# First four up units of the convolutional MLP computed in two passes over the row tiles, with five unread matmuls ahead of them

## The chip, the cores and the metric

The kernel runs on one core of a Trainium2 chip. The metric is the device time of one execution in microseconds (us). All engines work from their own in-order instruction streams and meet at semaphores: TensorE (PE, with its weight loads as PEld), VectorE (DVE), ScalarE (ACT), GpSimd (POOL) and SyncE (SP), which here only issues DMAs.

## What is computed

One layer (layer 0) on a sequence of 256 rows of width 2048, in float32: a mixer (mLSTM), then a gated MLP, each behind an RMS norm with a shift and a scale that come from a conditioning vector, and each added back with a gate.

```
sh1, sc1, g1, sh2, sc2, g2 = split(silu(c) @ w_mod + b_mod, 6)
x = x + g1 * mlstm_mixer(rms_norm(x) * (1 + sc1) + sh1)
hf = rms_norm(x) * (1 + sc2) + sh2
u = hf @ w_up                                   # 2048 -> 2 * 5632 columns
u = sum(pad(u)[:, j:j + 256] * conv_w[j] for j in range(3)) + conv_b
gate, val = split(u, 2)
x = x + g2 * ((silu(gate) * val) @ w_down)      # 5632 -> 2048
```

## The kernel before

**Split products.** Each float32 product is made from rounded halves. A weight tile in `raw` is rounded by ACT into `w_hi` (line 609) and DVE subtracts to make `w_lo` (line 975); the activations are split likewise into `hm_hi` and `hm_lo`, which lie side by side in `hm`. A row tile k is 128 of the 2048 rows of a weight matrix.

**Up units.** One unit is 128 output columns of `w_up`, that is 16 row tiles of 128x128, 1 MB. It has two halves of 8 row tiles. Units come in fours: gate and value columns of two pairs. Unit r of a four sums into PSUM bank 4 + r. Per row tile PE runs one matmul with 512 columns (`w_hi` against `hm_hi` and `hm_lo`, `up_hi`, line 1285) and one with 256 columns (`w_lo` against `hm_hi`, `up_lo`, line 1291). In the texts unit 0 is the first up unit, unit 4 the first of the second four, and so on.

**Buffers.** `raw` holds four units. `w_hi` and `w_lo` hold four halves each. ACT rounds a half when PE has finished the one four halves earlier (`half_done`). SP loads a unit into `raw` when DVE has finished both halves of the unit that lay there (`raw_done`).

**What ACT and DVE do for each unit.** ACT copies half of the bank to `up_sum` (line 930), DVE adds the other half (1241), ACT applies the middle tap and bias (935), DVE adds two taps (1245, 1250). After a pair ACT has applied Silu to the gate (925) and DVE multiplies (`act_hi`, 1257), POOL does the low part (589, 593). Between these steps stand the roundings and subtractions of coming weight halves, in a fixed order. Once in four units DVE also adds one row tile of the modulation matrix for g2 (`add_g2`, 1224, 128x2048), which SP loads (448) and which must be done before SP issues the next such load.

**Entry of the MLP.** PE ends the mixer's output projection, sums columns of `acc` (1395), transposes the last quarter of x (1552), and spreads the row of 1/rms over all partitions (1587). DVE then multiplies each row tile of x by it (`normalise`, 1201), ACT adds the shift and rounds (`hm_hi`, 892), DVE makes `hm_lo` (`shift_lo`, 1206). PE takes row tile k as soon as it is there: `first_up_units` runs units 0 and 1 together, k from 0 to 15, then `up_unit` runs units 2 and 3, then a loop runs fours. In the first pass of DVE's loop `add_g2` stands at r == 2, ahead of the addition for unit 2.

Of the kernel before, what the change touches and what calls it, by code (L numbers as in the profile page):

```python
# [5 lines left out]
def hybrid_mlstm_convffn_adaln_kernel(nc, x_d, c_d, w_mod, b_mod, w_in, gate_bias, h_norm, w_out,  # L6
# [5 lines left out]
    ds = bass.ds  # L12
# [44 lines left out]
    PAIR0 = F_TILE  # L57


    C_SH1, C_SC1, C_G1, C_SH2, C_SC2, C_G2 = (D * n for n in range(6))  # L60
# [31 lines left out]
    with ExitStack() as ctx:  # L92
# [242 lines left out]
        def _(sp):  # L335
# [263 lines left out]
        def _(act):  # L599
            def split_hi(v, plus=0):  # L600

                if v >= 2 * N_UNITS:
                    return
                if v < V_OUT:
                    act.wait_ge(half_in[v % 8], 16 * (v // 8 + 1))
                elif v % 2 == 0:

                    act.wait_ge(raw_in[v // 2 % 4], 16 * ((v - V_OUT) // 8 + 1) + 2 * plus)
                nc.scalar.activation(w_hi[:, v % 4, :], raw_half(v), ACT.Copy).then_inc(w_hi_made, 1)  # L609

            def slot_hi(p):
# [291 lines left out]
            def seed_y(n, q):  # L903
# [6 lines left out]
                for t in range(TB):  # L910
                    nc.scalar.activation(ps[:, 2 * (q % 2) + t, :],
                                         y_acc[:, t, q * QUARTER:(q + 1) * QUARTER], ACT.Copy)\
                             .then_inc(y_seeded, 1)

            for n, tiles in enumerate(CHUNKS):
                with act.Fori(0, tiles // 2) as i:
                    for r in range(4):
# [51 lines left out]
        def _(dve):  # L969
            def split_lo(v, plus=0):  # L970

                if v >= 2 * N_UNITS:
                    return
                dve.wait_ge(w_hi_made, v + 1 + plus)
                nc.vector.tensor_tensor(w_lo[:, v % 4, :], raw_half(v),  # L975
                                        w_hi[:, v % 4, :].bitcast(f32), ALU.subtract)\
                         .then_inc(raw_done, 1)

# [191 lines left out]
            for f in range(31):  # L1170
                split_lo(V_OUT + f + 3)
                attend(V_OUT + f - V_VO)
# [24 lines left out]
            split_lo(V_OUT + 34)  # L1197

# [13 lines left out]
            for k in range(KT + 2):  # L1212
                if k < KT:
                    normalise(k)
                if k >= 2:
                    shift_lo(k - 2)
                if k == 4:
                    split_lo(V_OUT + 35)

            def add_g2(tile, plus):  # L1220
# [5 lines left out]
                                               op0=ALU.mult, op1=ALU.add).then_inc(mod_done, 1)  # L1226

            for n, tiles in enumerate(CHUNKS):
                with dve.Fori(0, tiles // 2) as i:
                    for r in range(4):  # L1230
                        u, k = U_UP[n] + r, r // 2
                        w = 2 * F_TILE[n] + r
                        pair = F_TILE[n] + k
                        buf = (conv_val if r % 2 else conv_gate)[:, k, :]
                        col = 2 * i + (FT if r % 2 else 0) + pair
# [3 lines left out]
                        dve.wait_ge(low_taken, 4 * i + w + 1)  # L1239
                        total = up_sum[:, r % 2, :]  # L1240
                        nc.vector.tensor_tensor(total, ps[:, 4 + r, 0:SEQ], total, ALU.add)\
                                 .then_inc(up_made, 1)
                        split_lo(2 * u + 5, 8 * i)
                        dve.wait_ge(conv_base, 4 * i + w + 1)
                        nc.vector.scalar_tensor_tensor(out=buf[:, 1:SEQ], in0=total[:, 0:SEQ - 1],
                                                       scalar=cvT[:, ds(col + 2 * FT, 1)],
                                                       in1=buf[:, 1:SEQ], op0=ALU.mult, op1=ALU.add)\
                                 .then_inc(tap1_made, 1)
                        dve.wait_ge(tap1_made, 4 * i + w + 1)
                        nc.vector.scalar_tensor_tensor(out=buf[:, 2:SEQ], in0=total[:, 0:SEQ - 2],  # L1250
                                                       scalar=cvT[:, ds(col, 1)],
                                                       in1=buf[:, 2:SEQ], op0=ALU.mult, op1=ALU.add)\
                                 .then_inc(conv_done, 1)
                        if r % 2:
                            dve.wait_ge(silu_made, 2 * i + pair + 1)
                            dve.wait_ge(conv_done, 4 * i + w + 1)
                            nc.vector.tensor_tensor(act_hi[:, ds((2 * i + k) * SEQ, SEQ)],  # L1257
                                                    conv_gate[:, k, :], conv_val[:, k, :], ALU.mult)\
                                     .then_inc(act_hi_made, 1)
                groups = tiles // 4  # L1260
# [17 lines left out]
        def _(pe):  # L1278
# [312 lines left out]
            def first_up_units(u):  # L1591

                pe.wait_ge(raw_done, RAW0 + 2 * u + 3)
                for k in range(KT):
                    pe.wait_ge(hm_made, KT + k + 1)
                    if k == KT // 2:
                        pe.wait_ge(raw_done, RAW0 + 2 * u + 4)
                    for r in range(2):
                        up_hi(r, 2 * (u + r) + k // (KT // 2), k)
                    for r in range(2):  # L1600
                        last = up_lo(r, 2 * (u + r) + k // (KT // 2), k, stop=(k == KT - 1))
                        if r == 0 and k in (KT // 2 - 1, KT - 1):
                            last.then_inc(half_done, 1)
                last.then_inc(half_done, 2)
# [59 lines left out]
```

## Time and profile before

| | us |
|---|---|
| median of 3 runs | 1191.35 |
| lowest and highest | 1190.84 and 1191.42 |
| the profiled execution | 1191.6 |
| its span, first to last instruction | 1189.9 |
| mean granted clock of TensorE | 0.986 |
| TensorE busy | 1164.7 (98% of the span) |
| VectorE busy | 915.8 (77%) |
| ScalarE busy | 629.7 (53%) |
| GpSimd busy | 160.8 (14%) |

Times in the trace count from the first instruction. A busy engine isn't always one at full pace: the clock that TensorE is granted is shown beside its busy time. Idle time of an engine that nobody waits for costs nothing. Matmuls overlap, so their pace is the distance of their starts, not their duration.

### The profile page before, as it was taken

Reading aid. Unit: us, or ns where it says so; the run is one execution under the profiler, and the core shown is the slowest. Engines: PE = TensorE matmul, PEld = TensorE weight load, DVE = VectorE, ACT = ScalarE, POOL = GpSimd, SP = SyncE. Lnnn points to the kernel's source line nnn. Section 1 sums busy time; section 2 is a strip of 40 time slices with the busy share of each in tenths; the row PEclk is TensorE's granted clock in tenths of the full one; section 3 lists DMA queues with packets and bytes.
Section 4 is the critical chain, followed back from the end, with each engine's and each line's share of the span. In section 5 each row is a group of like instructions: output and inputs, shape, how many; then the busy total and the mean of one; then the engine's idle time right before and its main releaser. Section 6 shows DMA issues by size and latency. Waiting matters only on the chain.

```text
span 1189.9 us, 17137 instructions
## 1 busy us (share of the span) xinstructions
PE 1164.7 (98%) x5890; PEld 995.7 (84%) x5890; DVE 915.8 (77%) x984; ACT 629.7 (53%) x915; POOL 160.8 (14%) x167
## 2 busy tenths in 40 slices
PE   5799999999999999999999999999999999999998
PEld 5788888888888888888888888888888888888887
DVE  5799877989889988988886446888885456777654
ACT  4355565665654546555554445455454555555442
POOL 0000030111112320112211000211211000221200
PEclk9599999999999998999999999999999999999999
DMA  9999989999999993897875578789775566666552
GB/s 363 398 401 402 391 288 333 358 404 401 346 352 347 401 301 101 253 251 216 254 235 193 196 216 240 215 231 253 221 222 201 191 198 179 194 192 180 204 175 77
DMA packets 260440, 314.54 MB, mean 264 GB/s; under 512 B 6208, under 2 KB 186888, under 8 KB 251688
## 3 DMA queue, kind: packets, MB, share of 16 engines
q1 hardware_dynamic: 259360, 312.51, 78.6%
q0 software_dynamic: 592, 1.22, 0.4%
q8 instruction: 28, 0.46, 0.2%
q10 hardware_dynamic: 442, 0.21, 0.1%
q14 instruction: 18, 0.15, 0.0%
HBM read 311.80 MB, written 2.11 MB: 264 GB/s over the span
## 4 chain that ended last, share of the span: by engine, by line
PE 95%; DMA 2%; SPq 1%; DVE 1%; POOL 0%; ACT 0%; issue 0%; DVEq 0%
PE ps L1285 27%; PE ps L1291 14%; PE ps L1325 9%; PE ps L1327 9%; PE ps L1326 9%; PE ps L1372 8%; PE ps L1374 7%; PE ps L1373 7%; DMA m<-in_l_w_mod_dram 2%; PE ps L1395 1%; SPq L373 1%; DVE acc L1005 0%; POOL small L543 0%; PE ps L1501 0%; PE ps L1455 0%; PE ps L1343 0%
## 5 line engine op out<-in xcount | busy, mean ns | idle before, releaser
L975 DVE TENSOR_TENSOR w_lo<-raw,w_hi 128x1024 fp32r<-128x1024 f32 x392 | 482.2, 1232 | 179.6 <-ACT w_hi L609 177.8
L609 ACT ACTIVATE w_hi<-raw 128x1024 fp32r<-128x1024 f32 x392 | 414.4, 1057 | 359.2 <-PE ps L1327 165.4
L1285 PE MATMUL ps<-hm,w_hi 128*128 128x512 f32 x1408 | 340.8, 392 | 1.8 <-DVE hm L1206 1.8
L1285 PEld LDWEIGHTS ps<-hm,w_hi 128*128 128x128 f32 x1408 | 258.8, 189 | 50.9 <-issue 2.0
L1291 PEld LDWEIGHTS ps<-hm,w_lo 128*128 128x128 f32 x1408 | 183.7, 192 | 8.8 <-DVE w_lo L975 0.2
L1291 PE MATMUL ps<-hm,w_lo 128*128 128x256 f32 x1408 | 186.0, 283 | 0.0
L1372 PE MATMUL ps<-w_hi,hm 128*128 128x512 f32 x384 | 155.0, 404 | 3.2 <-DVE hm L1025 2.7
L1374 PE MATMUL ps<-w_hi,hm 128*128 128x512 f32 x384 | 150.5, 392 | 0.0
L1373 PE MATMUL ps<-w_lo,hm 128*128 128x512 f32 x384 | 150.3, 391 | 0.0
L1327 PE MATMUL ps<-w_hi,act_lo 128*128 128x512 f32 x344 | 133.8, 389 | 0.0
L1326 PE MATMUL ps<-w_lo,act_hi 128*128 128x512 f32 x344 | 133.8, 389 | 0.0
L1325 PE MATMUL ps<-w_hi,act_hi 128*128 128x512 f32 x344 | 133.8, 389 | 0.0
L589 POOL TENSOR_TENSOR act_full<-conv_gate,conv_val 128x256 f32<-128x256 f32 x44 | 32.6, 740 | 555.7 <-DVE conv_val L1250 555.7
L930 ACT ACTIVATE up_sum<-ps 128x256 f32<-128x256 f32 x88 | 33.5, 380 | 106.5 <-PE ps L1285 104.2
L1372 PEld LDWEIGHTS ps<-w_hi,hm 128*128 128x128 f32 x384 | 72.7, 189 | 19.4 <-DVE hm L1025 2.8
L1373 PEld LDWEIGHTS ps<-w_lo,hm 128*128 128x128 f32 x384 | 72.7, 189 | 15.4 <-issue 1.0
L1374 PEld LDWEIGHTS ps<-w_hi,hm 128*128 128x128 f32 x384 | 72.5, 189 | 15.7
L987 DVE SCALAR_TENSOR_TENSOR acc<-mod_raw,cT,acc 128x2048 f32<-128x2048 f32 x32 | 76.1, 2377 | 7.0 <-issue 4.4
L1326 PEld LDWEIGHTS ps<-w_lo,act_hi 128*128 128x128 f32 x344 | 64.6, 188 | 13.5
L1327 PEld LDWEIGHTS ps<-w_hi,act_lo 128*128 128x128 f32 x344 | 64.6, 188 | 13.4
L1325 PEld LDWEIGHTS ps<-w_hi,act_hi 128*128 128x128 f32 x344 | 64.6, 188 | 13.3
L593 POOL TENSOR_TENSOR act_lo<-act_full,act_hi 128x256 f32 x44 | 65.1, 1479 | 23.7 <-DVE act_hi L1257 23.7
(172 smaller groups left out, 1085.4 us busy)
## 6 DMA issues: line engine op xcount, KB each, us to landing
raw<-in_l_w_up_dram SPq DMA_DIRECT2D x88, 1024.0 KB, 5.8
raw<-in_l_w_in_dram SPq DMA_DIRECT2D x96, 512.0 KB, 11.9
mod_raw<-in_l_w_mod_dram SPq DMA_DIRECT2D x48, 1024.0 KB, 7.9
raw<-in_l_w_down_dram SPq DMA_DIRECT2D x44, 1024.0 KB, 5.0
m<-in_l_w_mod_dram SPq DMA_DIRECT2D x32, 640.0 KB, 13.6
raw<-in_l_w_out_dram SPq DMA_DIRECT2D x16, 1024.0 KB, 8.8
m<-in_l_w_mod_dram SPq DMA_DIRECT2D x16, 768.0 KB, 13.3
mod_third<-in_l_w_mod_dram SPq DMA_DIRECT2D x8, 1024.0 KB, 8.4
```

The lines of the kernel that those rows point to most:

```text
L593: nc.gpsimd.tensor_tensor(act_lo[:, part], act_full[:, k, :], act_hi[:, part].bitcast(f32), ALU.subtract)\
L609: nc.scalar.activation(w_hi[:, v % 4, :], raw_half(v), ACT.Copy).then_inc(w_hi_made, 1)
L975: nc.vector.tensor_tensor(w_lo[:, v % 4, :], raw_half(v), w_hi[:, v % 4, :].bitcast(f32), ALU.subtract)\
L987: nc.vector.scalar_tensor_tensor(out=part, in0=src, scalar=cT[:, ds(tile, 1)], in1=part, op0=ALU.mult, op1=ALU.add).then_inc(mod_done, 1)
L1285: return mm(ps[:, 4 + w % 4, :], w_hi[:, v % 4, j * P:(j + 1) * P], both, start=(k == 0), stop=stop, skip_group_check=True)
L1291: return mm(ps[:, 4 + w % 4, 0:SEQ], w_lo[:, v % 4, j * P:(j + 1) * P], hm_hi[:, k, :], start=False, stop=stop, skip_group_check=True)
L1325: mm(out, s_hi, hi, start=first, stop=False, skip_group_check=True)
L1326: mm(out, s_hi, lo, start=False, stop=False, skip_group_check=True)
L1327: last = mm(out, s_lo, hi, start=False, stop=final, skip_group_check=True)
L1372: mm(out, s_hi, hi, start=(k == 0), stop=False, skip_group_check=True)
L1373: mm(out, s_hi, lo, start=False, stop=False, skip_group_check=True)
L1374: last = mm(out, s_lo, hi, start=False, stop=(k == final), skip_group_check=True)
```

## The change

1. **PE, five unread matmuls** of 128x512 (`o_hi` by `o_hi`, into bank 5) stand behind the spread of the 1/rms row.
2. **PE, two passes.** Units 0 and 1 together on row tiles 0 to 7 (`two_units(0, 0)`), then unit 2 and unit 3 on row tiles 0 to 7 (`unit_half`), then the same on 8 to 15. For row tile 0 the 512 columns are two matmuls of 256, so that `hm_hi` is used before `hm_lo` is there.
3. **ACT and DVE, order of halves.** The first eight halves are split in the order 0, 2, 4, 6, 1, 3, 5, 7 (`FIRST_HALVES`, `first_hi`, `first_lo`). Eight, not five, are split before the loop of fours.
4. **ACT and DVE, first pass taken out of the loop** (`take_up`, `convolve`): the four units' sums are taken one after the other with one half to split in each, and `add_g2(0, 0)` comes behind the fourth.
5. **SP**: the loads of units 4 to 7 wait for the first four second halves; the order of loads is the same.

```
-            with sp.Fori(0, KT // 2 - 1) as i:
+            load_g2(0)
+            for r in range(4):
+                sp.wait_ge(raw_done, RAW0 + V_UP + 5 + r)
+                load(U_UP[0] + 4 + r, a_src(w_up, 2 * P + P * (r // 2) + (F if r % 2 else 0)), KT)
+            with sp.Fori(1, KT // 2 - 1) as i:
...
+            def first_hi(c):
+                act.wait_ge(half_done, V_UP + c - 3)
...
             for f in range(33):
                 if f == 31:
                     squares(3, 0)
+                if f < 29:
+                    slot_hi(V_OUT + f)
+                else:
+                    first_hi(f - 29)
                 if f == 32:
                     squares(3, 1)
                     take_z(3)
                     scale_shift(4, 12, ps[:, 1, 0:KT], shift_p[:], False)
                     act.wait_ge(sc_made, 6)
-                slot_hi(V_OUT + f)
...
+                if k in (9, 10):
+                    first_hi(k - 5)
+            first_hi(6)
+            first_hi(7)
...
-                if k == 4:
-                    split_lo(V_OUT + 35)
+                if k in (4, 10, 11):
+                    first_lo({4: 3, 10: 4, 11: 5}[k])
+            first_lo(6)
+            first_lo(7)
...
+            for r in range(4):
+                take_up(0, r, 0)
+                split_lo(V_UP + 8 + r)
+                convolve(0, r, 0)
+            add_g2(0, 0)
...
             last.then_inc(rstd_row, 1)
+            for _ in range(5):
+                mm(ps[:, 5, :], o_hi[:, 0:P], o_hi[:, 0:QUARTER], start=True, stop=True)
...
-            first_up_units(U_UP[0])
-            for r in range(2, 4):
-                up_unit(U_UP[0] + r, r)
+            two_units(0, 0)
+            unit_half(2, 2, 0)
+            unit_half(3, 3, 0)
+            two_units(4, KT // 2)
+            unit_half(6, 2, KT // 2)
+            unit_half(7, 3, KT // 2)
+            pe.wait_ge(up_made, 1)
```

**Order on PE, behind the spread row.** Before:

```order
L1587 MATMUL ps<-rstd_diag,ones 128x128 [waits o_made,diag_made]
L1587 MATMUL ps<-rstd_diag,ones 128x128
L1285 MATMUL ps<-hm,w_hi 128x512 [waits hm_made,raw_done,y_scaled]
L1285 MATMUL ps<-hm,w_hi 128x512
L1291 MATMUL ps<-hm,w_lo 128x256 x2
```

Now, at the same place:

```order
L1651 MATMUL ps<-rstd_diag,ones 128x128 [waits o_made,diag_made]
L1651 MATMUL ps<-rstd_diag,ones 128x128
L1654 MATMUL ps<-o_hi 128x512 x5
L1667 MATMUL ps<-hm,w_hi 128x256 [waits hm_hi_made,raw_done,y_scaled]
L1355 MATMUL ps<-hm,w_lo 128x256
L1667 MATMUL ps<-hm,w_hi 128x256
L1355 MATMUL ps<-hm,w_lo 128x256
L1667 MATMUL ps<-hm,w_hi 128x256 [waits hm_made]
```

The five matmuls fill the place in which PE waited, and row tile 0 starts on `hm_hi` alone.

**Order on DVE, end of the first four units.** Before (L1257 is `act_hi` of the first pair, L1224 `add_g2`, L1241 the addition for unit 2, all in the loop's body):

```order
L1257 TENSOR_TENSOR act_hi<-conv_gate,conv_val 128x256
L974 REGISTER_ALU
L975 TENSOR_TENSOR w_lo<-raw,w_hi 128x1024 [waits w_hi_made]
L1222 ISA [waits acc_ready1]
L1223 REGISTER_ALU [waits mod_in0]
L1224 REGISTER_ALU [waits mod_done]
L1224 SCALAR_TENSOR_TENSOR acc<-mod_raw,cT,acc 128x2048
L1239 REGISTER_ALU
L1241 TENSOR_TENSOR up_sum<-ps,up_sum 128x256 [waits low_taken]
```

Now (L1283 is the addition for unit 3, L1304 `act_hi` of the second pair, L1275 `add_g2`, and behind the branch stands the loop's first split, the first half of unit 6):

```order
L1283 TENSOR_TENSOR up_sum<-ps,up_sum 128x256 [waits low_taken]
L1014 TENSOR_TENSOR w_lo<-raw,w_hi 128x1024 [waits w_hi_made]
L1292 SCALAR_TENSOR_TENSOR conv_val<-up_sum,cvT,conv_val 128x255 [waits conv_base]
L1297 SCALAR_TENSOR_TENSOR conv_val<-up_sum,cvT,conv_val 128x254 [waits tap1_made]
L1304 TENSOR_TENSOR act_hi<-conv_gate,conv_val 128x256 [waits conv_done,silu_made]
L1275 SCALAR_TENSOR_TENSOR acc<-mod_raw,cT,acc 128x2048 [waits mod_done,mod_in0,acc_ready1]
L1315 UNCONDITIONAL_BRANCH
L1315 ISA
L1014 TENSOR_TENSOR w_lo<-raw,w_hi 128x1024 [waits w_hi_made]
```

`add_g2` has moved from between the two pairs to behind both, directly ahead of the split of unit 6.

**Order on SP, first loads of the MLP.** Before:

```order
L346 DMA raw<-in_l_w_up_dram 128x16x128 [waits raw_done] x4
L457 UNCONDITIONAL_BRANCH
L457 ISA
L448 ISA [waits mod_done]
L448 DMA mod_raw<-in_l_w_mod_dram 128x2048
```

Now:

```order
L349 DMA raw<-in_l_w_up_dram 128x16x128 [waits raw_done] x4
L451 DMA mod_raw<-in_l_w_mod_dram 128x2048 [waits mod_done]
L349 DMA raw<-in_l_w_up_dram 128x16x128 [waits raw_done] x4
L464 UNCONDITIONAL_BRANCH
L464 ISA
L451 ISA [waits mod_done]
L451 DMA mod_raw<-in_l_w_mod_dram 128x2048
```

The second load for g2 (the last row) waits for the first `add_g2`, and the load of unit 8 stands behind it, as before.

## Rows read from the trace of the kernel before

**Rows 1.** The page: the chain of work that ended last, shares by engine.

```profile
PE 95%; DMA 2%; SPq 1%; DVE 1%; POOL 0%; ACT 0%; issue 0%; DVEq 0%
```

**Rows 2.** Timeline, 440 to 480 us, at PE's wait: start, duration, instruction, [idle before].

```profile
449.27 1.06 ACT L609 ACTIVATE w_hi<-raw 128x1024 fp32r<-128x1024 f32 x1
449.61 1.08 DVE L1201 TENSOR_TENSOR hm_full<-hm_full,ps 128x256 f32<-128x256 f32 x3
450.24 1.88 ACT L892 ACTIVATE hm<-hm_full,shift_p 128x256 fp32r<-128x256 f32 x4
450.76 0.48 DVE L1206 SCALAR_TENSOR_TENSOR hm<-hm_full,shift_p,hm 128x256 fp32r<-128x256 f32 x1
...
451.39 1.19 PE L1285 MATMUL ps<-hm,w_hi 128*128 128x512 f32 x2 [1.82 <-DVE hm L1206]
...
456.99 0.48 DVE L1206 SCALAR_TENSOR_TENSOR hm<-hm_full,shift_p,hm 128x256 fp32r<-128x256 f32 x1
```

**Rows 3.** Windows: stretch, length, busy PE, PEld, DVE, ACT, POOL, PEclk, DMA share, GB/s.

```profile
450.50:451.00 0.50, 0.00 (x0) 0.00 (x0) 0.43 (x2) 0.50 (x2) 0.00 (x0) 0.50 0.00 0
...
457.00:457.50 0.50, 0.50 (x4) 0.40 (x3) 0.50 (x3) 0.39 (x1) 0.00 (x0) 0.99 1.14 347
```

**Rows 4.** The chain that ended last, 430 to 520 us: start, length, work.

```profile
453.01 0.85 PE ps L1285 x2
...
474.72 3.65 PE ps L1285 x16
478.37 0.95 PE ps L1291 x8
479.36 1.21 PE ps L1291 x8
```

**Rows 5.** Timeline of ACT ahead of the entry.

```profile
446.21 0.63 ACT L851 ACTIVATE sq_junk<-x 128x512 f32<-128x512 f32 x1 [1.04 <-DVE x L1188]
```

**Rows 6.** Timeline, 461 to 476 us: the steps of one pair of units.

```profile
465.28 0.38 ACT L930 ACTIVATE up_sum<-ps 128x256 f32<-128x256 f32 x1 [2.35 <-PE ps L1291]
...
465.70 0.42 DVE L1241 TENSOR_TENSOR up_sum<-ps,up_sum 128x256 f32<-128x256 f32 x1 [1.51 <-ACT up_sum L930]
...
466.65 1.23 DVE L975 TENSOR_TENSOR w_lo<-raw,w_hi 128x1024 fp32r<-128x1024 f32 x1 [0.52 <-ACT w_hi L609]
...
467.79 0.48 DVE L1245 SCALAR_TENSOR_TENSOR conv_gate<-up_sum,cvT,conv_gate 128x255 f32<-128x255 f32 x1
...
468.42 0.48 DVE L1250 SCALAR_TENSOR_TENSOR conv_gate<-up_sum,cvT,conv_gate 128x254 f32<-128x254 f32 x1
...
468.94 0.42 ACT L925 ACTIVATE conv_gate<-conv_gate 128x256 f32<-128x256 f32 x1 [0.89 <-DVE conv_gate L1250]
...
469.26 0.36 ACT L930 ACTIVATE up_sum<-ps 128x256 f32<-128x256 f32 x1
...
473.07 0.88 DVE L1257 TENSOR_TENSOR act_hi<-conv_gate,conv_val 128x256 f32 x1 [0.21 <-DVE conv_val L1250]
473.88 1.21 DVE L975 TENSOR_TENSOR w_lo<-raw,w_hi 128x1024 fp32r<-128x1024 f32 x1
```

**Rows 7.** Timeline, 468 to 500 us: PE's last piece of the four units; `add_g2`.

```profile
474.55 3.82 PE L1285 MATMUL ps<-hm,w_hi 128*128 128x512 f32 x16
475.01 2.82 DVE L1224 SCALAR_TENSOR_TENSOR acc<-mod_raw,cT,acc 128x2048 f32<-128x2048 f32 x1
477.76 0.41 DVE L1241 TENSOR_TENSOR up_sum<-ps,up_sum 128x256 f32<-128x256 f32 x1
...
478.09 1.21 DVE L975 TENSOR_TENSOR w_lo<-raw,w_hi 128x1024 fp32r<-128x1024 f32 x1
```

**Rows 8.** The page's DMA issues (KB each, median us to landing), and a window.

```profile
raw<-in_l_w_up_dram SPq DMA_DIRECT2D x88, 1024.0 KB, 5.8
raw<-in_l_w_in_dram SPq DMA_DIRECT2D x96, 512.0 KB, 11.9
...
480.00:485.00 5.00, 5.00 (x29) 4.35 (x29) 4.41 (x7) 4.39 (x7) 0.65 (x1) 1.00 0.99 324
```

More of the change, by code:

```diff
@@ L57, in hybrid_mlstm_convffn_adaln_kernel @@
     PAIR0 = F_TILE
+    V_UP = 2 * U_UP[0]
+    FIRST_HALVES = [2 * r for r in range(4)] + [2 * r + 1 for r in range(4)]
     C_SH1, C_SC1, C_G1, C_SH2, C_SC2, C_G2 = (D * n for n in range(6))
@@ L913, in seed_y @@
                              .then_inc(y_seeded, 1)
+            for r in range(4):
+                act.wait_ge(half_done, V_UP + 5 + r)
+                if r % 2:
+                    act.wait_ge(conv_done, r)
+                    nc.scalar.activation(conv_gate[:, r // 2, :], conv_gate[:, r // 2, :], ACT.Silu)\
+                             .then_inc(silu_made, 1)
+                if r >= 2:
+                    act.wait_ge(conv_done, r - 1)
+                nc.scalar.activation(up_sum[:, r % 2, :], ps[:, 4 + r, SEQ:2 * SEQ], ACT.Copy)\
+                         .then_inc(low_taken, 1)
+                split_hi(V_UP + 8 + r)
+                act.wait_ge(up_made, r + 1)
+                col = (FT if r % 2 else 0) + r // 2
+                nc.scalar.activation((conv_val if r % 2 else conv_gate)[:, r // 2, :], up_sum[:, r % 2, :],
+                                     ACT.Identity, bias=cvT[:, ds(col + 3 * 2 * FT, 1)],
+                                     scale=cvT[:, ds(col + 2 * 2 * FT, 1)]).then_inc(conv_base, 1)
             for n, tiles in enumerate(CHUNKS):
-                with act.Fori(0, tiles // 2) as i:
+                with act.Fori(int(n == 0), tiles // 2) as i:
                     for r in range(4):
@@ L1170, in _ @@
             for f in range(31):
-                split_lo(V_OUT + f + 3)
+                if f < 29:
+                    split_lo(V_OUT + f + 3)
+                else:
+                    first_lo(f - 29)
                 attend(V_OUT + f - V_VO)
@@ L1228, in _ @@
+            for r in range(4):
+                take_up(0, r, 0)
+                split_lo(V_UP + 8 + r)
+                convolve(0, r, 0)
+            add_g2(0, 0)
             for n, tiles in enumerate(CHUNKS):
-                with dve.Fori(0, tiles // 2) as i:
+                with dve.Fori(int(n == 0), tiles // 2) as i:
                     for r in range(4):
[L1231 to L1235, printed above, removed]
+                        u = U_UP[n] + r
@@ L1238, in _ @@
                             add_g2(n * KT // 2, i)
[L1239 to L1242, printed above, removed]
+                        take_up(n, r, i)
                         split_lo(2 * u + 5, 8 * i)
[L1244 to L1259, printed above, removed]
+                        convolve(n, r, i)
                 groups = tiles // 4
@@ L1588, in _, with two_units @@
             last.then_inc(rstd_row, 1)
+            for _ in range(5):
+                mm(ps[:, 5, :], o_hi[:, 0:P], o_hi[:, 0:QUARTER], start=True, stop=True)
             pe.wait_ge(y_scaled, 4 + 8)
-            def first_up_units(u):
-                pe.wait_ge(raw_done, RAW0 + 2 * u + 3)
-                for k in range(KT):
+            def two_units(c, k0):
+                pe.wait_ge(raw_done, RAW0 + V_UP + c + 2)
+                for k in range(k0, k0 + KT // 2):
+                    if k == 0:
+                        pe.wait_ge(hm_hi_made, KT + 1)
+                        for part in range(2):
+                            if part == 1:
+                                pe.wait_ge(hm_made, KT + 1)
+                            for r in range(2):
+                                mm(ps[:, 4 + r, part * SEQ:(part + 1) * SEQ], w_hi[:, r, 0:P],
+                                   hm[:, 0, part, :], start=(part == 0), stop=False,
+                                   skip_group_check=True)
+                                if part == 0:
+                                    up_lo(r, r, 0)
+                        continue
@@ L1603, in first_up_units, with unit_half @@
+                        if k == k0 + KT // 2 - 1:
                             last.then_inc(half_done, 1)
-                last.then_inc(half_done, 2)
+            def unit_half(c, r, k0):
+                pe.wait_ge(raw_done, RAW0 + V_UP + c + 1)
+                for k in range(k0, k0 + KT // 2):
+                    up_hi(r, c, k)
+                for k in range(k0, k0 + KT // 2):
+                    last = up_lo(r, c, k, stop=(k == KT - 1))
+                last.then_inc(half_done, 1)
             act_hi3 = act_hi[:].rearrange("p (k t) -> p k t", k=16)
```

43 lines of the change are left out of this document (37 added, 6 removed).

## Prediction

> **What bounds the kernel now.** First the profile page: PE is busy for 98% of the span and carries 95% of the chain that ended last [rows 1], so a microsecond won or lost on PE is one in the total, wherever it lies. Then the timeline at the MLP's entry. It shows PE's one large wait of the late kernel: the first up matmul starts at 451.39 after 1.82 us idle, so since 449.57, ended by DVE's hm_lo of row tile 0 [rows 2]. The windows show what follows: the granted clock is 0.50 (1.2 GHz) from 450.5 at the latest, with PE idle, and back at 0.99 (2.4 GHz) from 457.0 [rows 3]. The chain [rows 4] gives the pace: two 512-column matmuls take 0.85 us at 1.2 GHz, so with two of half the columns a row tile of two units takes 1.28; at full clock 16 of the 512-column ones take 3.65 (0.228 each), 8 of the 256-column ones 0.95 (0.12 each). So a half unit is 8 x 0.348 = 2.78 us, a unit 5.57.
>
> **The entry, part by part.** The profiled execution took 1191.6, with a span of 1189.9; the median of the runs is 1191.35, 0.25 less. I sum against the profile and take off 0.25.
>
> *Row tile supply.* ACT's rounding of the fourth half ran at 449.27 and held ACT until 450.24 [rows 2]. It now stands ahead of the squares, where ACT was idle for 1.04 us waiting for x [rows 5], and that cover just holds its slot of 0.97. So hm_hi of row tile 0 comes some 0.2 us earlier, and DVE's run of row tiles starts 0.15 earlier (its three normalisations, 1.08 from 449.61, become the limit). Row tile 7 ended at 456.99 + 0.48 = 457.47; now 457.32.
>
> *PE.* The five unread matmuls take 5 x 0.228 = 1.14 us, until 450.7, inside the old idle time; they cost nothing and delay nothing, since hm_hi of row tile 0 is ready only then. If the clock holds, PE waits for row tiles, since eight of them for two units are 8 x 0.70 = 5.6 us and come at 0.73 apart, with DVE's subtraction of half 3 (1.2 us) between tiles 2 and 3. It starts row tile 7 at 457.32 + 0.15 (DVE to PE: 451.24 to 451.39, rows 2) and ends at 458.15. **If the clock falls at 450.2 all the same**, for as long as PE takes to be busy again, the loss is mostly inside these waits: at half pace PE would reach row tile 2 by 454.4, when tile 3 has just come. So the unread matmuls matter less than they seem.
>
> From 458.15 everything left of the four units is 2 x 2.78 + 5.57 + 2 x 2.78 = 16.7 us: unit 4 starts at 474.86. Halves 4 to 7 are split by about 460.6, 462.5, 467.7 and 468.9; PE wants them at 463.7 (both of the pair), 469.3 and 472.1, so nothing is late. Before, unit 4 started in the middle of the x16 piece, at 474.55 + 8 x 0.228 = 476.38 [rows 7]. **Gain at the entry 1.5 us.** It isn't the 1.8 idle plus some 2.7 lost to the slow clock, as DVE's supply of row tiles is the next limit.
>
> *ACT and DVE behind it.* Here I see the price. Before, the sums of unit 0 were whole at 465.2, and DVE's addition ran at 465.70. Now unit 0 ends with the pair of second halves, at 458.15 + 5.57 + 5.57 = 469.29; the addition runs at +0.08 +0.42 = 469.8 [rows 6]. From there the same steps follow at the same distances, with fewer splits between, but each waits for ACT in turn. From rows 6: addition to w_lo 0.95, to tap one 1.14, to tap two 0.63, to Silu 0.52, to the next up_sum copy 0.32, to the addition 0.42: 3.98 for unit 0. Unit 1: 0.95 + 1.14 + 0.63 + 0.69 (0.48 of tap two and the 0.21 before act_hi) + 0.81 = 4.22. Unit 2, whose w_lo is ready at once (0.33, rows 7): 0.33 + 1.14 + 0.63 + 0.52 + 0.32 + 0.42 = 3.36. Unit 3 again 4.22. Then add_g2 holds DVE for 2.75 (475.01 to 477.76, rows 7), and only behind it stands the w_lo of unit 6's first half, 1.22, plus 0.15 to PE: 469.8 + 3.98 + 4.22 + 3.36 + 4.22 + 2.75 + 1.37 = 489.7.
>
> PE wants it earlier. The second half of unit 5 is due at 474.86 + 5.57 + 2.78 = 483.2; its w_lo is the one behind unit 3's addition (481.36 + 0.95 + 1.37 = 483.7): **stop of 0.45**. Unit 6 is due 2.78 later, 486.45: **stop of 3.25**. Before, the nearest thing was the 1.21 in place of 0.95 us at 479.36 [rows 4], 0.25, behind the old place of add_g2; that stop goes.
>
> *SP.* The next g2 load waits for add_g2, so it went out after 477.83 (475.01 + 2.82, rows 7); now it goes out at about 488.4 + 0.3, and the load of unit 8 is queued behind it, 489.1. ACT's rounding of that half, and all that ACT and DVE do behind it, wait for the landing. A lone 1 MB load lands 5.8 us after its issue [rows 8]; with the g2 load's 1.05 MB ahead of it at 324 GB/s (3.2 us) I take 498.1. Then 1.1 for w_hi, 1.13 for w_lo, 2.75 for the second add_g2, 0.33 for the addition and 1.37 for the w_lo of unit 8's second half: 504.8, due at 489.7 + 11.14 + 2.78 = 503.6. **Stop of 1.25.** Its bounds: none when the two loads don't slow each other (landing 494.9, ACT and DVE are busy with unit 5 until 497), 4.1 when unit 8's load takes the 11.9 us of the loads in the saturated part. The single-load row is the nearer. Behind that the lead comes back: DVE was busy for only 4.41 of 5.00 us there [rows 8], so it gains on PE.
>
> The Trainium skill (DMA: Bandwidth & Descriptors, Anatomy of one DMA) puts about 2.0 us of fixed cost on a DMA, mostly receipt, beside bytes over bandwidth. With this trace's 324 GB/s it gives 488.7 + 2.0 + 6.5 = 497.2 and, an estimate, a last stop of 0.35 instead of 1.25. For one load the row has 5.8 us where the rule of the Trainium skill gives 5.2, so I stay with the row.
>
> *Nil by cover:* PE's wait for the first addition (469.8 + 0.4, wanted at 474.86); loads of units 4 and 5, now issued near 461 and 463, landing near 467 and 470, wanted at 469.7 and 475.4.
>
> **Sum:** -1.5 - 0.25 + 0.45 + 3.25 + 1.25 = +3.2 us. 1191.6 + 3.2 - 0.25 = **1194.5**.
>
> **Rivals.**
> A. The sum above: 0.48 (with its bounds 1193.8 to 1195.6).
> B. The last stop doesn't come, because the two loads overlap: +1.9, 1193.3, with its bounds 1192.3 to 1193.7. For it: the old g2 load and the load of unit 8 followed each other too, and ACT shows no wait for them. 0.20.
> C. DVE isn't late, the other side. The steps of rows 6 hold waits on ACT (0.52 before w_lo, 0.89 at Silu) in loop code with register instructions; in straight code they could shrink. If unit 6's w_lo is ready for PE by 486.0 instead of 489.7, only the entry's gain is left: -1.75, **1189.6**. It must save 3.7 of the 19.9 us since 469.8, while the waits of rows 6 end with another engine's work and not with issue. 0.14.
> D. The unread matmuls don't do what they are for and the clock stays at 0.50 until 457.0, as before. Then PE leaves the first pass 1.2 us later: at 1.28 us a row tile from 451.2 it has done four and a half by 457.0, and the rest takes 3.5 x 0.70, until 459.4. All stops behind it stay, since DVE waits for the same sums: +4.4, 1195.7. Against it: the clock came back at 457.0 after PE had worked from 451.39, and here it works from 449.5 on. 0.13.
> E. Something not in the rows, either way: 0.05.
>
> The Trainium skill (TensorE: Matmul & The Clock Gate, Part 1: The HAM clock gate) says that the moment of the clock's change isn't tied to the kernel, so that one kernel shows different counts of slow matmuls from run to run. By it D's 1.2 us would come in some executions and not in others; this is why D keeps 0.13 although the rows speak against it.
>
> **How the numbers follow.** A measurement of this kernel tells about 0.2% (2.4 us) from no change, so slower begins at 1193.7 and faster ends at 1189.0. Slower: A 0.47, D 0.13, a part of B and E 0.04: 0.64. Faster: a part of C with more than its sum, 0.03, and E: 0.04. Same: the rest, 0.32. The range must leave out at most 0.2: it drops C and the far end of the last stop, and runs from B's low bound, widened by 0.4 for the chain's steps, 1191.9, to 1196.4 (D with some of the last stop's bound).
>
> **What would show it.** Right: PE without a wait over 0.6 us from 454.6 to 483; DVE's last row tile of the first eight near 457.3; unit 4 near 474.9; then PEld or PE waiting about 3 us near 486 to 490 for w_lo, with the 128x2048 step of DVE ending just before; the next g2 load near 488.5; a second wait near 504. Wrong: no wait at 486 (C); a clock of 0.50 to 457 (D); unit 4 at 476 (the entry isn't limited as I say).

## The result

| | us, median | lowest to highest | runs |
|---|---|---|---|
| kernel before | 1191.37 | 1190.84 to 1192.64 | 6 |
| changed kernel | 1195.42 | 1194.92 to 1197.61 | 6 |

The ratio is 1.0037, with a 95% interval of 1.0027 to 1.0048. The changed kernel is slower by some 4 us, against a forecast of 1194.5.

The profile of this comparison was of the changed kernel's slowest execution (1197.61, span 1195.9; the other five spans are 1193.2 to 1193.9). A second profile, taken with the experiments (e9, below: 1196.6, span 1194.9), shows the same kernel without the early fall of the clock at the entry. I read the stages in the second one and come back to the first for the clock.

In both the last stretch of PE already starts late, ahead of everything that was changed: the first column sums, which stood at 444.57 before, start at 445.31 and 445.89. So I compare distances from these sums. On that scale 1.32 us are to be taken off the second profile's times to lay them beside the rows of before.

The page of the changed kernel (first profile), chain by engine, beside [rows 1]:

```profile
PE 93%; DMA 2%; DVE 2%; SPq 1%; ACT 1%; POOL 0%; issue 0%; DVEq 0%; ACTq 0%
```

PE's share fell from 95% to 93% and DVE's rose from 1% to 2%. The end is now set for a while by VectorE. The timeline of PE in the second profile shows where (start, duration, instruction, idle before it and what ended it):

```profile
450.65 1.41 PE L1654 MATMUL ps<-o_hi 128*128 128x512 f32 x5
...
459.56 2.01 PE L1349 MATMUL ps<-hm,w_hi 128*128 128x512 f32 x8
...
476.31 2.00 PE L1349 MATMUL ps<-hm,w_hi 128*128 128x512 f32 x8
...
485.22 1.21 PE L1355 MATMUL ps<-hm,w_lo 128*128 128x256 f32 x8 [0.39 <-DVE w_lo L1014]
...
491.16 2.50 PE L1349 MATMUL ps<-hm,w_hi 128*128 128x512 f32 x8 [2.89 <-DVE w_lo L1014]
```

The row at 459.56 is unit 2's first half, so the first pass over units 0 and 1 ends there. Unit 4 starts at 476.31, 30.42 us behind the column sums; before it was 476.38 - 444.57 = 31.81 [rows 7]. That is the gain, 1.39 us. Unit 5's second half waits at 485.22 and unit 6 at 491.16, and there the gain is lost twice over. The timeline of DVE up to that second wait:

```profile
471.22 0.43 DVE L1283 TENSOR_TENSOR up_sum<-ps,up_sum 128x256 f32<-128x256 f32 x1 [0.99 <-ACT up_sum L945]
...
475.13 0.42 DVE L1283 TENSOR_TENSOR up_sum<-ps,up_sum 128x256 f32<-128x256 f32 x1 [0.82 <-ACT up_sum L945]
...
479.25 0.41 DVE L1283 TENSOR_TENSOR up_sum<-ps,up_sum 128x256 f32<-128x256 f32 x1
...
483.00 0.43 DVE L1283 TENSOR_TENSOR up_sum<-ps,up_sum 128x256 f32<-128x256 f32 x1 [0.82 <-ACT up_sum L945]
...
487.10 2.34 DVE L1275 SCALAR_TENSOR_TENSOR acc<-mod_raw,cT,acc 128x2048 f32<-128x2048 f32 x1
489.37 1.74 DVE L1014 TENSOR_TENSOR w_lo<-raw,w_hi 128x1024 fp32r<-128x1024 f32 x1
```

These are the four additions of the peeled units (3.91, 4.12 and 3.75 apart), then `add_g2`, then unit 6's split, which PE waits for. That is the chain [rows 6, 7] were read for. After the stop the clock goes down, in the windows of the same profile (columns as in [rows 3]):

```profile
491.00:492.00 1.00, 0.84 (x4) 0.71 (x5) 1.00 (x3) 0.29 (x1) 0.00 (x0) 1.00 0.42 123
492.00:493.00 1.00, 1.00 (x5) 0.81 (x4) 0.97 (x2) 1.00 (x2) 0.00 (x0) 0.84 0.99 418
493.00:494.00 1.00, 1.00 (x5) 0.87 (x4) 0.88 (x2) 0.62 (x3) 0.00 (x0) 0.50 0.98 411
```

PE stood still until 491.16, its clock fell within 492 to 493, when it was busy again, and stayed at 0.50 (1.2 GHz) to 496.

Unit 6's first half and the first eight matmuls of its second, 24 in all, take 3.86 us from start to start at full clock (488.31 to 492.17 in e10, below); here 491.16 to 496.54 is 5.38. So the fall costs 1.52 us. The prediction had no such term.

The transfers behind it, timeline of SyncE's queue and of ACT in the second profile:

```profile
489.70 0.37 SPq L451 DMA_DIRECT2D mod_raw<-in_l_w_mod_dram  x1
490.42 4.34 SPq L349 DMA_DIRECT2D raw<-in_l_w_up_dram  x2
```

```profile
499.58 1.06 ACT L616 ACTIVATE w_hi<-raw 128x1024 fp32r<-128x1024 f32 x1 [3.72 <-DMA raw<-in_l_w_up_dram]
```

The load for unit 8 goes out at 490.42 and ACT waits 3.72 us for it. Yet PE has no wait at unit 8 here, since the slow clock has put it back by more than the data are late.

**The sum by this profile**, in starts of PE against starts: -1.39 (entry), -0.28 (the old stop at 479.36, [rows 4]), +0.54 (unit 5: its eight matmuls start at 485.22 and not at 484.68), +3.07 (unit 6: 491.16 against 488.09), +1.52 (clock) = +3.5. Further on the starts of PE are 3.69 later than before (507.68 - 445.89 against 502.67 - 444.57), so some 0.2 us is in none of these terms. The medians differ by 4.05 in the first comparison and by 3.69 in the second (1195.07 against 1191.38). The terms are those of one execution, though: how often the clock falls behind the stop in the others isn't shown, so the share of the clock in the median isn't fixed by it.

The first profile differs in one thing. Its clock fell at the entry too, in the windows:

```profile
448.00:449.00 1.00, 1.00 (x10) 1.00 (x9) 0.21 (x2) 0.88 (x3) 0.72 (x1) 0.74 0.00 0
...
454.00:455.00 1.00, 1.00 (x7) 1.00 (x6) 1.00 (x4) 0.79 (x2) 0.00 (x0) 0.50 0.00 0
455.00:456.00 1.00, 1.00 (x7) 0.92 (x7) 1.00 (x2) 0.07 (x1) 0.00 (x0) 0.85 0.00 0
```

It fell during the second column sums, before the unread matmuls, which then took 2.48 us in place of 1.41 and ended as late as 454.0. Unit 4 started 31.99 us behind the first sums (477.30 - 445.31), so the entry gained nothing in that execution. It explains most of why it was 2 us above the rest.

### The profile page after: what moved, and what is told of

It is laid out like the page before. It is cut to its first block, busy times and chain, and to the rows that moved or that the text cites. A ratio compares the mean times of both kernels' runs of the same rounds, so it can differ in the third digit from the quotient of the medians.

```text
span 1195.9 us, 17083 instructions
## 1 busy us (share of the span) xinstructions
PE 1167.4 (98%) x5897; PEld 997.6 (83%) x5897; DVE 916.7 (77%) x984; ACT 629.2 (53%) x915; POOL 158.7 (13%) x167
## 3 DMA queue, kind: packets, MB, share of 16 engines
q0 software_dynamic: 592, 1.22, 0.4%
## 4 chain that ended last, share of the span: by engine, by line
PE 93%; DMA 2%; DVE 2%; SPq 1%; ACT 1%; POOL 0%; issue 0%; DVEq 0%; ACTq 0%
PE ps L1349 26%; PE ps L1355 14%; PE ps L1389 9%; PE ps L1391 9%; PE ps L1390 9%; PE ps L1436 8%; PE ps L1438 7%; PE ps L1437 7%; DMA m<-in_l_w_mod_dram 2%; PE ps L1459 1%; SPq L376 1%; DVE w_lo L1014 1%; DVE acc L1051 0%; ACT w_hi L616 0%; POOL small L550 0%
## 5 line engine op out<-in xcount | busy, mean ns | idle before, releaser
L1014 DVE TENSOR_TENSOR w_lo<-raw,w_hi 128x1024 fp32r<-128x1024 f32 x384 | 473.2, 1234 | 181.4 <-ACT w_hi L616 179.3
L616 ACT ACTIVATE w_hi<-raw 128x1024 fp32r<-128x1024 f32 x384 | 406.0, 1058 | 359.1 <-PE ps L1391 162.9
```

The costliest lines, as they stand in the source:

```text
L1014: nc.vector.tensor_tensor(w_lo[:, v % 4, :], raw_half(v), w_hi[:, v % 4, :].bitcast(f32), ALU.subtract)\
```

## The experiments

My theory after the two profiles: the interleaved first pass is a gain; what makes the kernel slower is one stop at unit 6, made by the chain of sums and by `add_g2` ahead of that unit's split, and the fall of the clock that the stop brings. The rivals: the entry itself (unread matmuls, clock); the chain of sums alone or the addition alone; the late transfer of unit 8. All comparisons are with runs of the kernel before on the same chip (medians 1191.41, 1191.22 and 1191.38, of 27, 33 and 15 runs). The experiments are told by question and not in the order of their numbers.

**e9: the changed kernel again, for a second profile.**

> The changed kernel as it is, for a second profile: the first was its slowest execution, with the clock at 0.50 from 448.48 to 455.30. Theory: in an execution in which the clock stays up through the entry, unit 4 starts 30.4 us behind the first column sums (31.8 before), the stops of 0.38 and 2.88 us at units 5 and 6 stand as they are, and the clock falls in the latter for about 3.4 us; 1195.0 to 1195.8. Rival: without the fall at the entry the second does not come either, and the stop at unit 8's second half is there instead.

Measured: 1195.07 (1194.46 to 1197.53, 5 runs), ratio 1.0036, interval 1.0022 to 1.005. The rows above are from it. Unit 4 came at 30.42, the stops were 0.39 and 2.89, the clock fell for 3.4 us behind them, and no wait at unit 8. The rival is out: here the second fall came without the first.

**e1: `add_g2` moved ahead of the sums.**

```diff
+            add_g2(0, 0)
             for r in range(4):
                 take_up(0, r, 0)
                 split_lo(V_UP + 8 + r)
                 convolve(0, r, 0)
-            add_g2(0, 0)
```

> The changed kernel with VectorE's one add_g2(0, 0) moved from behind the four peeled sums to ahead of them, behind first_lo(7), where VectorE waits 1.00 us for PE anyway. Theory (the addition that stands directly ahead of unit 6's w_lo makes the long stop, and the stop makes the clock fall again): the stop of 2.88 us at unit 6 shrinks to about 0.5, stops of 0.4 and 1.2 come at unit 5 (the sums start 1.4 later), the next row of modulation weights is asked for earlier, so unit 8 does not wait either, and the clock is not at 0.50 near 493: -2.88 +0.5 +1.2 -1.7 = about -2.9, 1192 to 1192.6 us. Rival 1 (the entry, with its five unread matmuls and the interleaved first pass, costs the time): 1195 to 1196, no change. Rival 2 (the chain of sums itself is too slow, whatever stands ahead of unit 6): the stops at units 5 and 6 sum to 3 us or more and the time stays above 1194.5.

Measured: 1191.54 (1190.94 to 1192.84, 11 runs), ratio 1.0000, interval 0.9991 to 1.0009. One instruction in another place takes back the whole loss, a little more than the 1192 to 1192.6 that I expected. Timeline of PE in e1, its wait at unit 5's second half and unit 6 behind it:

```profile
483.87 1.22 PE L1355 MATMUL ps<-hm,w_lo 128*128 128x256 f32 x8 [0.95 <-DVE w_lo L1014]
484.93 4.20 PE L1349 MATMUL ps<-hm,w_hi 128*128 128x512 f32 x16
```

The stop of 2.89 has gone. Left are 0.95 and about 0.4 inside the x16 group, which takes 4.20 where an undisturbed one takes 3.82. The clock did not fall:

```profile
486.00:487.00 1.00, 0.93 (x5) 0.43 (x3) 1.00 (x2) 0.00 (x0) 0.90 (x1) 1.00 1.05 296
488.00:489.00 1.00, 1.00 (x6) 0.79 (x6) 1.00 (x2) 1.00 (x2) 0.00 (x0) 1.00 1.08 279
```

So rivals 1 and 2 fall: neither the entry nor the sums alone keep the time up. Why e1 only equals the kernel before can be added up from starts: the entry gains 1.40 (unit 4 at 474.40 - 443.99 = 30.41) and the old stop 0.28, and against that stand 1.10 at unit 5's second half (483.87, due at 482.77), 0.10 behind it and 0.39 in the x16 group (from start to start 4.04 in place of 3.65).

**e4: PE kept busy through the stop.**

```diff
+            for r in range(4):
+                if r == 2:
+                    for _ in range(12):
+                        mm(ps[:, 0, :], hm[:, 0, 0, 0:P],
+                           hm[:, 0, :, :].rearrange("p a t -> p (a t)"), start=True, stop=True)
+                up_unit(U_UP[0] + r, r, 8)
             for n, tiles in enumerate(CHUNKS):
-                with pe.Fori(int(n == 0), tiles // 2) as i:
+                with pe.Fori(2 * int(n == 0), tiles // 2) as i:
```

> The changed kernel with twelve unread matmuls of 512 columns on PE between unit 5 and unit 6, in the stop of 2.88 us (12 x 0.228 = 2.74 us), into bank 0 that nothing reads then; the loop of the up units starts one turn later for it, and nothing else moves. Theory (the clock falls because PE stood still for 2.88 us): no 0.50 near 493, which gives back about 1.7 us, and in its place unit 8's second half waits about 1.25 us for its late transfer, as forecast: 1195.4 - 1.7 + 1.25 = about 1195.0, with the stop at unit 8 in the trace. Rival 1 (the clock falls there for another reason, at every run): it falls all the same, 1195.4. Rival 2 (unit 8's data are in time): 1193.7.

Measured: 1193.86 (1193.08 to 1196.03, 11 runs), ratio 1.0018, interval 1.0009 to 1.0027. The work that PE waits for ends as late as before: unit 6 starts 45.27 us behind the first sums (490.97 - 445.70), as in e9 (491.16 - 445.89). Timeline of PE, then a window behind it:

```profile
487.91 2.88 PE L1702 MATMUL ps<-hm 128*128 128x512 f32 x12
490.97 2.11 PE L1349 MATMUL ps<-hm,w_hi 128*128 128x512 f32 x8 [0.18 <-DVE w_lo L1014]
```

```profile
493.00:494.00 1.00, 1.00 (x11) 1.00 (x10) 1.00 (x2) 0.62 (x3) 0.00 (x0) 1.00 0.92 367
```

The clock stays at 1.00, and the median is 1.2 us below that of e9 and 1.6 below that of the first comparison. The kernels ran on different chips, so the size is rough, but it agrees with the 1.52 us that the matmuls of unit 6 show. So the clock has a share in the loss, and with PE kept busy the fall doesn't come: rival 1 is out. That standing still always brings it is not so, as e10 shows next. The stop at unit 8 did not come in its place, and the time is that of rival 2. The load for unit 8 landed 7.9 us after its issue here (490.22 to 498.10), against 9.1 in e9; this one landing was 1.2 us quicker, and the traces don't show why.

**e10: the split of half 3 moved behind row tile 7, in the changed kernel.**

```diff
-                if k in (4, 10, 11):
-                    first_lo({4: 3, 10: 4, 11: 5}[k])
+                if k in (9, 10, 11):
+                    first_lo({9: 3, 10: 4, 11: 5}[k])
```

> The changed kernel with only first_lo(3) moved behind row tile 7 (k == 9 instead of 4). Theory (VectorE's supply bounds the first pass of the changed kernel, and PE's end of it starts the chain of sums, addition and split behind it): the first pass ends 1.0 to 1.1 us earlier and nearly all of it arrives, since the sums start earlier too (VectorE has 1.0 us of idle ahead of the first): -0.9 to -1.1 us, 1194.3 to 1194.6, with the stops at units 5 and 6 as they were. Rival (the stop at unit 6 ends when the addition and the split end, whatever PE gained ahead of it): the stop grows by what the entry gains, 1195.4.

Measured: 1194.33 (1192.75 to 1196.98, 11 runs), ratio 1.0026, interval 1.0017 to 1.0035. That is 0.74 below e9 on the same chip, within the spread of both. Its profile is of an execution of 1192.77, one of its fastest, in which the clock stayed up although the stop was the same. Timeline of PE, then a window behind the stop:

```profile
488.31 2.11 PE L1349 MATMUL ps<-hm,w_hi 128*128 128x512 f32 x8 [2.89 <-DVE w_lo L1014]
...
502.79 1.21 PE L1355 MATMUL ps<-hm,w_lo 128*128 128x256 f32 x8 [0.29 <-DVE w_lo L1014]
```

```profile
490.00:491.00 1.00, 1.00 (x9) 0.93 (x8) 0.85 (x3) 0.62 (x2) 0.00 (x0) 1.00 0.93 395
```

Unit 6 starts 44.11 us behind the first sums (488.31 - 444.20) and not 45.27: the stop has not grown, and the 1.16 us that the entry gained arrive. So the rival is out by the trace, though the medians alone wouldn't tell. Two more things follow. The stop of 2.89 brings the fall in some executions only. And where it doesn't come, the forecast wait at unit 8's second half is there, but it is 0.29 us of idle (0.45 from start to start: 502.79, due at 502.34) and not 1.25.

**e5 and e6: the sums in pairs.** ScalarE's and VectorE's steps of the peeled units, which take turns, are written two units at a time. In e5 `add_g2(0, 0)` stays behind them, in e6 it stands ahead. VectorE's side:

```diff
-            for r in range(4):
-                take_up(0, r, 0)
-                split_lo(V_UP + 8 + r)
-                convolve(0, r, 0)
+            for k in range(2):
+                take_up(0, 2 * k, 0)
+                take_up(0, 2 * k + 1, 0)
+                split_lo(V_UP + 8 + 2 * k)
+                convolve(0, 2 * k, 0)
+                split_lo(V_UP + 9 + 2 * k)
+                convolve(0, 2 * k + 1, 0)
```

ScalarE does the same: both copies of the low half, the first split, both bases, the second split, the Silu.

> The changed kernel with its four peeled sums interleaved in pairs, the one add_g2(0, 0) still behind them. ScalarE copies both low halves of a pair and makes both convolution bases before the second split, VectorE makes both sums first: in the kernel as changed each sum waits for ScalarE behind the taps of the one ahead (0.82 + 0.53 + 0.81 + 0.53 us of idle in the profile of g2_first, and 1.9 us on ScalarE at the third). Theory (the stop at unit 6 is the chain of sums plus the addition, and either is enough to shorten it): the sums end about 2.6 us earlier, the stop of 0.38 at unit 5 goes, that of 2.88 falls to about 0.5, the clock does not fall there, and unit 8's second half waits 0 to 1 us: 1195.4 - 0.4 - 2.4 - 1.6 + 0.5 = about 1191.5. Rival (the addition alone is the cause, the sums are not on the path): the stop falls by less than 1 us, 1194 or more.

Measured for e5: 1191.14 (1190.65 to 1193.96, 11 runs), ratio 0.9997, interval 0.9988 to 1.0006. The profile is of its slowest execution (1193.96), in which the clock fell early at the entry, as in the first profile, and unit 4 started 32.02 us behind the first sums. The sums and PE's wants behind them both move with that, so the stops can be compared. Timeline of PE, all its waits behind unit 4:

```profile
489.25 2.11 PE L1363 MATMUL ps<-hm,w_hi 128*128 128x512 f32 x8 [0.26 <-DVE w_lo L1025]
...
503.97 1.22 PE L1369 MATMUL ps<-hm,w_lo 128*128 128x256 f32 x8 [0.53 <-DVE w_lo L1025]
```

The stop at unit 6 fell from 2.89 to 0.26 with the addition where it was. So to take away either cause alone is enough: the long stop needs both. The rival, that the addition alone is the cause, is out. The second row is the wait at unit 8's second half again, 0.53.

> Both: the peeled sums in pairs and add_g2(0, 0) ahead of them. Theory: the stops of 0.95 and 0.4 us and the small one between, that g2_first still has at units 5 and 6, go (sum about 2.0 in my model of the steps, 1.4 to 2.0), since the second pair ends some 2.5 us earlier: 1191.5 - 1.4 to 2.0 = 1189.5 to 1190.1. Rival (the copies of unit 3's sum still wait for unit 3's last matmul and the stops only move to unit 6): 1191 or more.

Measured for e6: 1189.29 (1188.41 to 1192.42, 12 runs), ratio 0.9987, interval 0.9977 to 0.9996. The only wait that the table of PE's waits (what PE waited for, us, times, longest) still names between 440 and 600 us is at the entry:

```profile
PE ps L1363 <- DVE hm L1266: 0.2, 1, 0.2
```

With all stops gone the entry's gain arrives: the median is 1.9 us below the kernel before, and in the profile the starts of PE are 1.62 earlier, 1.34 from the entry (unit 4 at 474.43 - 443.96 = 30.47) and 0.28 from the old stop.

**e7: e6 and the split of half 3 behind row tile 7**, as in e10.

> As pairs_g2_first, and VectorE's first_lo(3), the 1.22 us split that stands between row tiles 2 and 3, moved behind row tile 7 (k == 9 instead of 4). Its result is read only by unit 3's first half, 2.8 us behind the first pass. Theory (VectorE's supply bounds the first pass, and this split is 1.13 us of it): PE's wait of 0.90 us ahead of row tile 3 goes, the first pass ends 1.0 to 1.1 us earlier, and nothing behind it is late: 1189.7 - 1.1 = about 1188.6. Rival (PE's own pace of 0.70 a row tile, or ScalarE, is as late): -0.3 or less.

Measured: 1188.51 (1187.80 to 1190.40, 9 runs), ratio 0.9976, interval 0.9967 to 0.9986. This is the fastest kernel of the study, 2.7 us below the kernel before. Its page has PE at 95% of the chain again:

```profile
PE 95%; DMA 2%; DVE 1%; SPq 1%; POOL 0%; issue 0%; ACT 0%; DVEq 0%
```

In its timeline of PE the first pass ends at 456.57, 12.53 us behind the first column sums of 444.04; in e9 it was 459.56 - 445.89 = 13.67:

```profile
456.57 2.01 PE L1363 MATMUL ps<-hm,w_hi 128*128 128x512 f32 x8
```

In e10, too, it is 12.53 (456.73 - 444.20). The 1.14 us are the split's slot on VectorE; PE's wait of 0.88 us ahead of row tile 3, which e9 has, is gone too. The median moved by 0.8 from e6.

**e2, e3 and e8: the five unread matmuls.** e2 is the changed kernel without them, e3 the kernel before with them in its wait, e8 is e7 without them.

```diff
-            for _ in range(5):
-                mm(ps[:, 5, :], o_hi[:, 0:P], o_hi[:, 0:QUARTER], start=True, stop=True)
```

> The changed kernel without its five unread matmuls behind the spread rows. Theory (VectorE's supply of row tiles bounds the first pass, the unread matmuls take no time and help only by bringing the clock back sooner): the clock comes back later than 455.3 on the profile's scale, the first pass runs behind VectorE by a little, +0 to +1.3 us: 1195.4 to 1196.7. Rival (the unread matmuls delay row tile 0 on PE, which starts only 0.2 us behind the last of them): -0.3 to -1 us, 1194.4 to 1195.1.

Measured for e2: 1198.01 (1195.10 to 1198.44, 5 runs), ratio 1.0041, interval 1.0028 to 1.0055. More than forecast. Windows:

```profile
448.00:449.00 1.00, 1.00 (x8) 1.00 (x7) 0.58 (x3) 1.00 (x4) 0.39 (x1) 0.59 0.00 0
...
457.00:458.00 1.00, 1.00 (x5) 0.82 (x4) 1.00 (x4) 0.75 (x2) 0.00 (x0) 0.50 0.00 0
458.00:459.00 1.00, 1.00 (x6) 0.85 (x6) 1.00 (x4) 0.60 (x2) 0.00 (x0) 0.79 0.00 0
```

The clock was down for some 10 us, and unit 4 started 32.75 us behind the first sums, against 30.42 with the unread matmuls in e9 and 31.99 with them and an early fall. All five executions had a mean clock of 0.983 to 0.985; of the changed kernel five of six had 0.987 to 0.989. The median is 2.6 to 2.9 us above that of the changed kernel, but that is not the price of the unread matmuls. Here the clock fell in the window 448 to 449, as it did in the first profile, ahead of the place where they stand, and they can't have prevented that. Against the first profile, like against like, the difference is 32.75 - 31.99 = 0.76 us: with them the clock was back near 455.3, without them near 458.8. Whether the other four executions fell early too is not recorded.

> The kernel before with only the five unread matmuls added, in its wait of 1.82 us at the entry. Theory (there each unit's row tile runs at half clock from 450.2 to 457.0, and VectorE's supply of 0.73 a tile lies close below PE's slow pace of 1.28): the clock stays up or comes back sooner, -0.3 to -1.2 us: 1190.2 to 1191.1, and the sums behind the entry show no stop above 0.5. Rival (the wait and not the clock is what the entry costs): 1191.4, within 0.2. Rival 2 (they end later than row tile 0 is ready): +0.3 to +0.8.

Measured for e3: 1191.28 (1190.30 to 1193.59, 11 runs), ratio 0.9998, interval 0.9989 to 1.0007: nothing that can be told. Its profile has the clock back between 452 and 453, where the kernel before had it near 457 [rows 3]:

```profile
452.00:453.00 1.00, 1.00 (x5) 0.81 (x5) 1.00 (x4) 0.71 (x2) 0.00 (x0) 0.69 0.00 0
453.00:454.00 1.00, 1.00 (x7) 0.83 (x6) 1.00 (x2) 0.00 (x0) 0.00 (x0) 1.00 0.00 0
```

The median is the rival's value (the wait and not the clock is what the entry costs). In that one execution the stretch from the sums to the late units is 1.0 us shorter than in the profile of before, but the medians don't bear it out; how much of the entry's slow clock the other executions of before had, I can't say.

> As e7_also_lo3_later without the five unread matmuls. Theory (they keep the clock up through the entry; without them the changed kernel lost 2.6 us in the median, of which about 1 us was clock in its profile and the rest the start of the clock): +1 to +2.6 us over e7. Rival (with a shorter entry they do nothing): within 0.5 of e7.

Measured for e8: 1189.62 (1187.40 to 1192.62, 12 runs), ratio 0.9987, interval 0.9977 to 0.9996. The median is 1.1 above e7, but its executions spread over 5.2 us where e7's spread over 2.6, and the lowest of e8 is below the lowest of e7. Neither profile has an early fall. In e8's the clock went down in PE's wait and was back near 454; unit 4, timelines of PE in e7 and in e8:

```profile
473.32 2.00 PE L1363 MATMUL ps<-hm,w_hi 128*128 128x512 f32 x8
```

```profile
474.70 2.00 PE L1363 MATMUL ps<-hm,w_hi 128*128 128x512 f32 x8
```

That is 29.28 us behind the first sums in e7 (444.04) and 30.02 in e8 (444.68), so 0.74 without the unread matmuls, as in e2. The medians of both pairs go the same way; that the matmuls lower the median by more than this, or narrow the spread, is not shown.

## Why the prediction was right, step by step

I lay the second profile on the rows of before by taking off 1.32.

- **Supply of row tiles.** Forecast: row tile 7 ready at 457.32, end of the first pass 458.15. Measured: 458.22 + 0.49 - 1.32 = 457.39 and 459.56 - 1.32 = 458.24. That this is VectorE's limit, with the split of half 3 in it, e10 and e7 show.
- **Gain at the entry.** Forecast 1.5, unit 4 at 474.86; measured 1.39 and 474.99. The point that the 1.8 idle and the slow clock don't add up to the gain held, since VectorE's supply is the next limit.
- **The unread matmuls.** "They cost nothing" held. "They matter less than they seem" held for their own part: two pairs of profiles show 0.76 us (e2 against the first profile) and 0.74 (e8 against e7), against the 1.82 us of idle time in whose place they stand. What I had not reckoned with is a fall ahead of them. It cost 1.57 us (31.99 against 30.42) although they were there.
- **The chain.** First addition 469.8, measured 469.90. The distances 3.98, 4.22, 3.36, 4.22 came as 3.91, 4.12, 3.75 and (to `add_g2`) 4.10. From `add_g2` to the split it was 2.27 and not 2.75, but from the split to PE 1.79 and not 1.37. Together that is 19.94 against 19.9: unit 6 at 489.84, forecast 489.7. The whole is right because errors of up to 0.5 us cancel, which is luck.
- **The stops.** Forecast 0.45 and 3.25; measured 0.54 and 3.07 from start to start. Rival C, that straight code would be quick enough, is out.
- **SyncE.** The next load of modulation weights was forecast for 488.5, unit 8's landing for 498.1; measured 488.38 and, on this scale, 498.24. The row for a single load plus the transfer ahead of it was the right guide for this execution: ACT took up the load for unit 8 9.0 to 9.2 us after its issue in four of five profiles (the first, e2, e9, e10). In e4 it was 7.9. The estimate by the Trainium skill (DMA: Bandwidth & Descriptors, Anatomy of one DMA), 497.2, was early for those four and near for e4 (498.10 - 1.13 = 496.97 on the scale of before). That section gives its fixed cost for transfers issued by GpSimd; the loads here are issued by SyncE, so they are no test of it.
- **The last stop: the mis-sized term.** Forecast 1.25 (its own addends give 504.8 - 503.6 = 1.2); measured 0.29 (e10), 0.53 (e5) and none (e4, with the quicker landing). From landing to PE I had 6.7 us, 6.55 of them to the ready split; in e9 the latter is 6.07 (499.56 to 504.41 + 1.22). Most of that is the second `add_g2`, which held VectorE for 2.26 (501.81 to 504.07) where I had 2.75 from [rows 7].
- **What was missing.** The sum had no fall of the clock behind a stop of 3 us, though [rows 3] show exactly this: a wait of 1.82 and then 0.50. I priced the clock where PE's waiting was removed and not where it was added. It costs 1.52 us in e9, and in the three profiles in which it comes behind the stop (the first, e9, e2) it covers the last stop. So the time was right to 0.9 us with one term of 1.25 too many and one of 1.5 too few. The mechanism of the stop was forecast; that these two nearly cancel in the sum is luck.
- **Rival B** (1193.3, no last stop) is near e4's 1193.9 in its outcome, and B had no fall of the clock behind the stop either. Its reason, two loads that don't slow each other, is not borne out: even there the landing took 7.9 us and not the 5.8 of a lone load. **Rival D** (the clock down at the entry) came in the first profile in another form: the fall began ahead of the unread matmuls, ended near 455.3 and cost 1.57 us, where D had the clock down to 457.0 and 1.2. The Trainium skill (TensorE: Matmul & The Clock Gate, Part 1: The HAM clock gate) says that the moment of the change isn't tied to the kernel; the two profiles of one kernel, down from 448.5 to 455.3 in one and not at all at the entry in the other, agree.

## What to carry to other kernels

Where units are finished together, their sums come in a bunch, and a long step of the same engine that stood harmlessly between them now stands ahead of the next thing PE needs: put it into the idle time ahead of the bunch, and write dependent steps of two engines two units at a time. Price a new stop of PE with the slow clock that can follow it, and not with its length alone: of the four profiles with a stop of 2.9 us three had it. Of a wait that is removed, look for the supply that is the next limit, and for work in that supply that nobody needs yet (here one split, 1.14 us).

## What was unexpected in the hardware

- The clock fell after the stop and not in it: PE worked again from 491.16 (e9) and the fall is in the window 492 to 493. The same stop of 2.89 us left the clock at 1.00 in the profile of e10. Why the one and not the other is open.
- The clock also fell while PE was busy without a gap with its column sums of one column each (first profile, 448 to 449; e2, e5 and e6 the same). What it costs goes with how long it stays down: in e6 it was back near 452, and unit 4 still came 30.47 us behind the first sums; in the first profile it was back near 455.3 and unit 4 came at 31.99, in e2 near 458.8 and 32.75.
- VectorE and GpSimd hold each other up, not in proportion but by turns. GpSimd's subtraction (timeline of POOL in the second profile) takes 0.74 us alone and 2.58 when it begins beside `add_g2`:

```profile
487.44 2.58 POOL L600 TENSOR_TENSOR act_lo<-act_full,act_hi 128x256 f32 x1 [0.54 <-DVE act_hi L1304]
...
498.89 0.74 POOL L600 TENSOR_TENSOR act_lo<-act_full,act_hi 128x256 f32 x1 [0.53 <-DVE act_hi L1304]
```

It ended at 490.02, some 0.6 us after `add_g2` (487.10 + 2.34 = 489.44), and VectorE's split that began at 489.37 took 1.74 in place of 1.22. The Trainium skill (SBUF — State Buffer, SBUF: two separate sides) describes the shared pair of ports as "an exclusive lock, not a bandwidth split"; the rows agree. In the profile of the kernel before, GpSimd was already at work when the `add_g2` of [rows 7] began at 475.01 (timeline of POOL):

```profile
474.22 1.47 POOL L593 TENSOR_TENSOR act_lo<-act_full,act_hi 128x256 f32 x1 [0.55 <-DVE act_hi L1257]
```

By the same reading its 2.82 would hold 0.47 of waiting (2.82 - 2.35), and this would be why 2.75 was too long a price for it elsewhere: a duration taken from a row includes who else was at work in it. No run here takes GpSimd's work away, so the lock itself is argued from such overlaps and not shown.
